# Attention heads of a hybrid transformer layer: 64-column value product and key projection in column pairs, row sums on GpSimd

## What is computed

```python
def mla_q(cq, q_norm_g, w_uq, cos, sin):
    q = (rms_norm(cq, q_norm_g) @ w_uq).reshape(B, S, MLA_HEADS, QK_NOPE + QK_ROPE)
    ...
def mla_kv(ckv, k_rope, kv_norm_g, w_ukv, cos, sin):
    kv = (rms_norm(ckv, kv_norm_g) @ w_ukv).reshape(B, S, MLA_HEADS, QK_NOPE + V_HEAD)
    k_nope, v = kv[..., :QK_NOPE], kv[..., QK_NOPE:]
    ...
def attend(q_nope, q_rope, k_nope, k_rope, v):
    s = jnp.einsum('bqhd,bkhd->bhqk', q_nope, k_nope) + jnp.einsum('bqhr,bkr->bhqk', q_rope, k_rope)
    p = jax.nn.softmax(s.astype(jnp.float32) * MLA_SCALE, axis=-1).astype(v.dtype)
    return jnp.einsum('bhqk,bkhd->bqhd', p, v)
```

## Time and profile before

| | us |
|---|---|
| median of 3 runs | 2931.52 (2930.42 to 2933.87) |
| profiled execution, its own time | 2926.87 |
| its span in the profile | 2925.0 |
| TensorE matmuls busy | 2750.9 (94%) |
| VectorE busy | 2183.4 (75%) |
| ScalarE busy | 1541.6 (53%) |
| GpSimd busy | 306.9 (10%) |

### The profile page before, as it was taken

One profiled execution on the slowest core, in us unless ns is written; L12 is line 12 of the kernel. 1 busy time (PEld: TensorE's weight loads), 2 busy tenths in 40 slices (PEclk: granted clock), 3 DMA queues, 4 the chain that ended last, 5 costly groups with the idle time before them and its releaser, 6 DMA issues. The chain is left out here.

```text
span 2925.0 us, 39328 instructions
## 1 busy us (share of the span) xinstructions
PE 2750.9 (94%) x13482; PEld 2111.5 (72%) x13482; DVE 2183.4 (75%) x2247; ACT 1541.6 (53%) x1486; POOL 306.9 (10%) x250
## 2 busy tenths in 40 slices
PE   5999998999998975999999999999999999999993
PEld 2765586678786544888888888888888888888882
DVE  1114357566662447999999999999999999999995
ACT  1212212333332113777777777777777777777774
POOL 0010000000001200111111111111111111111110
PEclk8999989999999987999999999999999999999996
DMA  6520002000002224666196699966966966669993
GB/s 252 195 101 1 1 0 74 6 5 6 3 1 80 88 90 174 201 201 201 29 337 205 207 378 378 378 205 216 363 201 215 359 201 202 233 205 377 376 335 136
DMA packets 223497, 527.53 MB, mean 180 GB/s; under 512 B 25938, under 2 KB 26195, under 8 KB 222323
## 3 DMA queue, kind: packets, MB, share of 16 engines
q1 hardware_dynamic: 206544, 475.31, 44.4%
q0 software_dynamic: 13968, 50.86, 7.4%
q10 hardware_dynamic: 2930, 0.62, 0.1%
HBM read 487.92 MB, written 38.81 MB: 180 GB/s over the span
## 5 line engine op out<-in xcount | busy, mean ns | idle before, releaser
L1883 DVE TENSOR_TENSOR wl<-w,wh 128x2048 fp32r<-128x2048 f32 x580 | 1301.4, 2284 | 26.9 <-ACT wh L1831 21.1
L1831 ACT ACTIVATE wh<-w 128x2048 fp32r<-128x2048 f32 x580 | 1111.7, 1917 | 291.1 <-PE PS L1744 291.1
L1744 PE MATMUL PS<-wh,xTh 128*128 128x512 f32 x1536 | 497.6, 405 | 4.0 <-DVE wl L1883 4.0
L1744 PE MATMUL PS<-wl,xTh 128*128 128x512 f32 x1536 | 474.9, 390 | 0.0
L1744 PE MATMUL PS<-wh,xTl 128*128 128x512 f32 x1536 | 474.3, 390 | 0.0
L1744 PEld LDWEIGHTS PS<-wh,xTh 128*128 128x128 f32 x1536 | 285.9, 189 | 68.2 <-DVE wl L1883 4.9
L1744 PEld LDWEIGHTS PS<-wl,xTh 128*128 128x128 f32 x1536 | 288.6, 188 | 61.8
L1744 PEld LDWEIGHTS PS<-wh,xTl 128*128 128x128 f32 x1536 | 288.6, 188 | 61.6
L1744 PE MATMUL PS<-wh,hTh 128*128 128x512 f32 x768 | 261.5, 421 | 0.0
L1723 POOL DMA_INDIRECT acc_dram<-hid,idxs x48 | 136.9, 2852 | 1089.9 <-DVE hid L1932 1089.9
L1744 PE MATMUL PS<-wh,hTl 128*128 128x512 f32 x768 | 241.0, 395 | 0.0
(11 more groups left out here) (329 smaller groups left out, 2993.1 us busy)
## 6 DMA issues: line engine op xcount, KB each, us to landing
w<-in_w_gu_dram SPq DMA_DIRECT2D x512, 512.0 KB, 9.1
w<-in_w_down_dram SPq DMA_DIRECT2D x128, 1024.0 KB, 10.5
later_wmod<-in_w_mod_dram SPq DMA_DIRECT2D x8, 2048.0 KB, 8.1
wmod<-in_w_mod_dram SPq DMA_DIRECT2D x8, 1024.0 KB, 13.7
w_mixer<-in_w_in_dram SPq DMA_DIRECT2D x8, 512.0 KB, 19.6
x<-in_x_dram SPq DMA_DIRECT2D x8, 512.0 KB, 3.4
w_out<-in_w_out_dram SPq DMA_DIRECT2D x1, 4096.0 KB
ox<-in_x_dram SPq DMA_DIRECT2D x8, 512.0 KB, 4.1
```

The source lines that it names most:

```text
L1744: mm = pe.matmul(PS[:, bank + g, :], op[:, k, :], ws[slot][:, kk, g, :], start=False, stop=(last and op is xs[1]))
L1831: act.activation(wh[c % SLOTS][:, :], w[c][:, :], ACT.Copy).then_inc(s_hi, 1)
L1883: dve.tensor_tensor(wl[c % SLOTS][:, :], w[c % NW][:, :], wh[c % SLOTS][:, :].bitcast(F32), ALU.subtract).then_inc(s_lo, 1)
```

## The change

The value product is turned round: the head's value tile (64 columns, now without the ones) is stationary and 512 columns of `probT` move; an even key tile writes output partitions 0 to 63, the odd one beside it 64 to 127. So each half ends with two partial sums, transposed. VectorE copies them to SBUF (`values_out`), and TensorE's `output_rows` adds and transposes them by a product with two stacked identities, and makes the row sums by a product of `acc` with a column of ones. `acc` is the sum of the ten `probT` tiles, made by nine additions on GpSimd for each half. `project_k` computes keys 0 to 639 in one column group and 640 to 1279 in the other, so `k_hi` and `k_lo` have two pieces. Exps wait until the old tile in their slot has been added. `max_rows(h,1)`, `max_hi(h,1)` and `max_lo(h,1)` move to later places, and the slots of the scores are new.

```diff
+            @block.gpsimd
+            def _(pool):
+                def add(h, half, op):
+                    done = 18 * h + (9 * half + op)
+                    pool.wait_ge(s_ex, h * NST + (NT * half + op + 2))
+                    if op:
+                        pool.wait_ge(s_acc, done)
+                        pool.tensor_tensor(acc[half][:, :], acc[half][:, :], probT[:, op + 1, :], ALU.add).then_inc(s_acc, 1)
+                    else:
+                        pool.tensor_tensor(acc[half][:, :], probT[:, 0, :], probT[:, 1, :], ALU.add).then_inc(s_acc, 1)
+                def body(h, j, more):
+                    for half in range(2):
+                        if not (isinstance(h, int) and h == 0):
+                            pool.wait_ge(s_ot, 2 * h + (half - 1))
+                        for op in range(9):
+                            add(h, half, op)
...
                 def k_hi(h, j):
                     act.wait_ge(s_kp, h + 1)
-                    act.activation(kTh[j][0:NOPE, :], flat[0:NOPE, 0:KEYS], ACT.Copy).then_inc(s_kh, 1)
+                    act.activation(kTh[j][0:NOPE, 0:KH], flat[0:NOPE, 0:KH], ACT.Copy)
+                    act.activation(kTh[j][0:NOPE, KH:], flat[NOPE:P, 0:KH], ACT.Copy).then_inc(s_kh, 1)
...
                         act.wait_ge(s_st, h * NST + (n + 1))
+                        if n >= NT or not (isinstance(h, int) and h == 0):
+                            act.wait_ge(s_acc, 18 * h + (9 * (n // NT) + max(n % NT, 1) - 9))
...
                 def body(h, j, more):
                     exps(h, 0, 8)
+                    max_hi(h, j, 1)
                     if more:
                         q_hi(h + 1, 1 - j)
                         k_hi(h + 1, 1 - j)
...
                     exps(h, NT + 7, NST)
-                    if more:
-                        max_hi(h + 1, 1 - j, 1)
...
+                def values_out(h, half):
+                    dve.wait_ge(s_pv, 2 * h + (half + 1))
+                    dve.tensor_copy(oT[:, :], PS[:, O0, :]).then_inc(s_ov, 1)
                 def output(h, half):
-                    dve.wait_ge(s_pv, 2 * h + (half + 1))
+                    dve.wait_ge(s_ot, 2 * h + (half + 1))
...
                 def body(h, j, more):
-                    max_lo(h, j, 1)
                     if not (isinstance(h, int) and h == 0):
+                        values_out(h - 1, 1)
                         output(h - 1, 1)
                     if more:
                         q_rope(h + 1)
...
                     mixer_square(h)
+                    max_lo(h, j, 1)
                     if more:
                         k_lo(h + 1, 1 - j)
-                        maxima(h + 1, 0, 3)
+                        maxima(h + 1, 0, 1)
+                    values_out(h, 0)
+                    if more:
+                        maxima(h + 1, 1, 3)
                     output(h, 0)
...
-                    for c, (lo, w) in enumerate(CH):
+                    for c, (lo, w) in enumerate(((0, 512), (512, KH - 512))):
                         for k in range(KVL // P):
-                            mm = pe.matmul(PS[0:NOPE, S0 + c, 0:w], wkh[j][:, k, :], m.ckvT[:, k, lo:lo + w],
-                                           start=(k == 0), stop=(k == KVL // P - 1))
+                            for e in range(2):
+                                mm = pe.matmul(PS[NOPE * e:NOPE * e + NOPE, S0 + c, 0:w], wkh[j][:, k, :], m.ckvT[:, k, KH * e + lo:KH * e + lo + w],
+                                               start=(k == 0), stop=(k == KVL // P - 1))
...
-                    pe.wait_ge(s_ex, h * NST + (NT * half + t + 1))
+                    pe.wait_ge(s_ex, h * NST + (NT * half + 2 * i + 2))
+                    for e in range(2):
+                        mm = pe.matmul(PS[VH * e:VH * e + VH, O0, :], v[j][:, 2 * i + e, :], probT[:, 2 * i + e, :],
+                                       start=(i == 0), stop=(i == NT // 2 - 1))
+                    if i == NT // 2 - 1:
+                        mm.then_inc(s_pv, 1)
+                def output_rows(h, half):
+                    pe.wait_ge(s_ov, 2 * h + (half + 1))
+                    pe.wait_ge(s_acc, 18 * h + (9 * half + 9))
                     for q in range(NQ // 2):
-                        mm = pe.matmul(outs[:, q, :], probT[:, t, q * P:(q + 1) * P], v[j][:, t, :],
-                                       start=(t == 0 and q == 0), stop=(t == NT - 1 and q == NQ // 2 - 1), skip_group_check=True)
+                        pe.matmul(outs[:, q, 0:VH], oT[:, q * P:(q + 1) * P], pair_i[:, :], start=True, stop=True)
+                    for q in range(NQ // 2):
+                        mm = pe.matmul(outs[:, q, VH:VH + 1], acc[half][:, q * P:(q + 1) * P], ones[:, :], start=True, stop=True)
+                    mm.then_inc(s_ot, 1)
...
                     if more:
                         project_q(h + 1, 1 - j)
+                    max_rows(h, 1)
+                    if not (isinstance(h, int) and h == 0):
+                        output_rows(h - 1, 1)
                     for n in range(8):
                         key_scores(h, j, n)
...
-                    todo = [(0, t) for t in range(NT)] + [(None, n) for n in range(NT, NST)] + [(1, t) for t in range(NT)]
-                    slot = {3: 0, 7: 1, 10: 2, 13: 3, 16: 4, 18: 5, 21: 6, 25: 7}
+                    todo = [(0, i) for i in range(NT // 2)] + [(None, n) for n in range(NT, NST)] + [(1, i) for i in range(NT // 2)]
+                    slot = {2: 0, 4: 1, 7: 2, 9: 3, 12: 4, 14: 5, 16: 6, 18: 7}
                     for n, (half, which) in enumerate(todo):
                         if more and n in slot:
                             scores(h + 1, 1 - j, slot[n])
-                        if more and n == 17:
+                        if n == 8:
+                            output_rows(h, 0)
+                        if more and n == 12:
                             max_rows(h + 1, 0)
...
-                    if more:
-                        max_rows(h + 1, 1)
```

More of the change, by code:

```diff
@@ L898, in phase_attention @@
             ("wkh0", [P, KVL // P, NOPE], F32), ("wkh1", [P, KVL // P, NOPE], F32),
-            ("negmax", [P, NQ], F32), ("rinv", [P, 2, NQ // 2], F32), ("cst", [P, SEQ], F32), ("qraw", [DQ, SEQ], F32), ("rtmp", [P, HALF], F32),
+            ("negmax", [P, NQ], F32), ("rinv", [P, 2, NQ // 2], F32), ("acc0", [P, HALF], F32),
+            ("pairI", [P, VH], F32), ("ones", [P, 1], F32), ("cst", [P, SEQ], F32), ("qraw", [DQ, SEQ], F32), ("rtmp", [P, HALF], F32),
             ("msv", [P, 4, MH], F32), ("msln", [P, MH], F32)])
-        m.attn, qTh0, qTh1, qTl0, qTl1, kTl1, wq0, wq1, wk0, wk1, negmax, rinv, cst, qraw, rtmp, msv, msln = items
+        m.attn, qTh0, qTh1, qTl0, qTl1, kTl1, wq0, wq1, wk0, wk1, negmax, rinv, acc0, pair_i, ones, cst, qraw, rtmp, msv, msln = items
         assert end <= m.R1
@@ L904, in phase_attention @@
             ("kTh0", [DQ + 1, KEYS], F32R), ("kTh1", [DQ + 1, KEYS], F32R), ("kTl0", [DQ + 1, KEYS], F32R)])
-        (probT, vall), at_end = m.run(end, [("probT", [P, NT, HALF], F32), ("vall", [P, NT, HEADS, VH + 1], F32)])
+        (probT, vall, acc1), at_end = m.run(end, [("probT", [P, NT, HALF], F32), ("vall", [P, NT, HEADS, VH], F32), ("acc1", [P, HALF], F32)])
+        oT = m.at("oT", [P, HALF], F32, m.tabs_at)
+        acc = (acc0, acc1)
+        KH = KEYS // 2
         assert at_end <= 229344
@@ L909, in phase_attention @@
         assert end + 4 * KVL // P * HEADS * VH <= m.R1 + 32768
-        (v0, v1), _ = m.run(m.after_w_out, [("v0", [P, NT, VH + 1], F32), ("v1", [P, NT, VH + 1], F32)])
+        (v0, v1), _ = m.run(m.after_w_out, [("v0", [P, NT, VH], F32), ("v1", [P, NT, VH], F32)])
         qTh, qTl, kTh, kTl, v, wqh, wkh = (qTh0, qTh1), (qTl0, qTl1), (kTh0, kTh1), (kTl0, kTl1), (v0, v1), (wq0, wq1), (wk0, wk1)
@@ L944, in _ @@
                 sp.wait_ge(s_wo, 16)
+            @block.gpsimd
[14 more added lines that the diff above has]
+                            add(h, half, op)
+                heads(pool, body)
             @block.scalar
@@ L994, in _ @@
                 max_hi(0, 0, 0)
-                max_hi(0, 0, 1)
                 def body(h, j, more):
                     exps(h, 0, 8)
+                    max_hi(h, j, 1)
                     if more:
@@ L1098, in _ @@
                 dve.wait_ge(s_krl, 2)
-                dve.memset(vall[:, :, :, VH:VH + 1], 1.0).then_inc(s_kr, 1)
+                dve.sem_inc(s_kr, 1)
+                for e in range(2):
+                    dve.tensor_copy(pair_i[64 * e:64 * e + VH, :], m.ident[64 * e:64 * e + VH, 64 * e:64 * e + VH])
+                dve.memset(ones[:, :], 1.0).then_inc(s_cs, 1)
                 dve.wait_ge(s_tab, 32)
@@ L1133, in _ @@
                 heads(dve, body)
+                values_out(HEADS - 1, 1)
                 output(HEADS - 1, 1)
@@ L2016, in build_program @@
         ("cs_tab", [P, NT, ROPE], F32), ("sn_tab", [P, NT, ROPE], F32)])
+    m.tabs_at = end - 2 * 4 * NT * ROPE
```

14 lines of the change are left out of this document (8 added, 6 removed).

## The result

The changed kernel took 2967.41 us (median of 4 runs, 2961.37 to 2977.76) against 2930.97 us (2926.19 to 2933.87) for the kernel before on the same chip: ratio 1.0130, 95% interval 1.0097 to 1.0162. It is slower by 36 us. The forecast was 2947, in a range of 2912 to 2970. Its profiled execution took 2969.58 us with a span of 2967.5.

A forecast was written before the change was run, and what follows sets the result against it. TensorE bounds the attention heads; the change moves the bound to VectorE's chain: 47.1 + 3.2 + 0.4 + 1.2 = 51.9 us a middle head. Six heads +18.8, head 0 +2, last -4.3, start -1.4: 2947 us, range 2912 to 2970.

The forecast's parts named there:

- The value product and the keys: TensorE per head: value product 8.6 us instead of 18.5, key projection 2.2 instead of 4.4; sum -8.4 with output rows.
- the forecast's likeliest case: Middle heads: bound moves to VectorE's chain, period 47.1, with contention and clock 51.9 us; total 2947; chance 0.47.
- the links: VectorE's chain of row maxima, each waiting for its scores: 2.44 us a link where nothing else stands between.
- The contention: VectorE operations waiting behind GpSimd's additions: 3.2 us a head on the way to the keys, 0.4 for q_lo and gate.
- The clock: Scores and two value pairs behind TensorE's 5 to 6 us gap may run at half speed: 1.2 us a head, 0 to 2.
- The last head: No scores chain, TensorE or GpSimd bound: 30.9 us plus 1 for GpSimd against 36.2 before, -4.3.
- Start and head 0: Stage start -1.4 us, from key projection and small operations; head 0, without output rows before it, 51.1 against about 49, +2.
- a small contention: Rival 1, middle heads: few VectorE operations wait and TensorE keeps its clock; period 47.3 to 48.2, 2914 to 2920; chance 0.27.
- one addition's time with the clock up: Rival 2, VectorE loses one addition in the whole train, clock stays: period 49.3, about 2931, no change; chance 0.15.
- TensorE as the bound: Rival 3, TensorE stays the bound because the assumed VectorE order is wrong: -8.4 x 8, 2865; chance 0.03.
- pairs that don't run side by side: Rival 4, value product needs 17 us, period above 56: 2980 or more; chance 0.03.
- the contention at its full price: Rival 5, the gate's small operations wait too and GpSimd is late at the last heads: 2968 to 2985; chance 0.05.

The follow-up runs named there:

- the filler: The changed kernel with 18 useless matmuls put into TensorE's 4.3 us wait for the second low part of the keys: 2950.62 us, 1.0063 of the kernel before.
- the reciprocal late: The changed kernel with the mixer's 3.34 us reciprocal moved behind the first maximum on VectorE: 2964.92 us, ratio 1.0069.
- the additions after the rotation: The changed kernel with mixer first and output late, GpSimd's first additions also waiting for the next head's rotated queries: 2911.79 us, ratio 0.9926.

## Why the prediction was right

**The value product and the keys, right.** Two pairs of tiles in 1.94 us (forecast 0.86 for each), key projection 2.38 (2.2), maxima rows and both kinds of output rows as the weight loads said. TensorE did stop being the bound, and the gain of 8.4 us a head was lost on VectorE's chain, as the forecast's likeliest case had it. That the period would fall only to 47.1 without contention and clock can be tested in two ways. With most additions left out, the four heads at the full clock took 48.3 us, of which 0.5 is the addition that was kept: 47.8. And with the parts that the runs isolate taken off the changed kernel's head (53.8 - 2.5 for the clock - 2.8 and 0.6 for GpSimd) it is 47.9. So the links are some 0.8 us a head longer than I had summed. Nearly all of it lies behind the keys; the way to the keys came out at 22.7 (25.5 - 2.8) against 22.75, with one slip in it: 8.1 and 0.75 make 8.85, not 9.05.

**The contention, right in size and mechanism.** Forecast 3.2 us on the way to the keys. Measured in the head shown, against the earlier trace rows: rotation 0.51 + 0.21, copy 0.77, gate's addition 1.08, small one 0.25, together 2.8. The keys were ready at 25.5 instead of the forecast 26. My picture of the train was half right: one copy and `L1102` paid, the second copy (0.17) and the square (0.67) not. The step that I had left open, whether a copy and an operation with one tensor and a constant are held, is settled: 0.19 became 0.96 and 0.42 became 1.50. The Trainium skill (SBUF — State Buffer, Who interferes with whom) says that a copy or an operation of this form, in a mode that uses two ports, contends with GpSimd for the pair of ports that the two engines share; the measurements agree, though not all seven operations of my upper end waited. In the last head, where GpSimd starts only at 918.51, `L1101` and `L1102` ahead of it took 0.68 and 0.42 again, as forecast. The addition itself was mis-sized: 1.28 us and 1.42 from one to the next, not 1.1, in proportion from 768 columns. In the middle heads that cost TensorE nothing, for it still lies within the cover of 2 us; in the last head it did.

**The clock, right in mechanism and wrong in size.** This is the term that failed in the middle heads. I took 1.2 us, between 0 and 2; the filler shows 2.5. It named the right work: two scores and two value pairs took 1.41, 3.68 and 1.38 us instead of the filler's 0.82, 1.94 and 0.85, together 2.9 us more. But I priced it as if VectorE's links hid half of that. The prediction's own walk had maximum 1 behind the copy of the values, and the copy behind the fifth pair, so nearly the whole lengthening lies on the chain. Six heads at 1.3 us more are 8 of the 11 us by which the middle heads were off. The remaining 3 us are the links (0.8 a head), less the 0.2 by which both terms for GpSimd together came out below 3.6.

**The last head, wrong.** Forecast -4.3, measured +2.1. Two terms failed here, the clock, which I had left at full speed, and the 1 us for GpSimd. (The items of the sum also add up to 29.9, not 30.9.) The clock first. In this head, in order of time:

```profile
913.15 1.81 PE L1258 MATMUL PS<-ones,acc 128*128 128x1 f32 x8
...
917.53 0.63 PE L1236 MATMUL PS<-qTh,kTh 97*128 97x512 f32 x1
...
933.27 0.78 PE L1236 MATMUL PS<-qTh,kTh 97*128 97x512 f32 x1
```

```profile
915.00:916.00 1.00, 1.00 (x3) 0.81 (x4) 0.96 (x3) 0.00 (x0) 0.00 (x0) 0.50 0.00 0
938.00:939.00 1.00, 1.00 (x4) 0.71 (x4) 0.00 (x0) 0.32 (x2) 0.86 (x2) 0.50 0.00 0
```

The key scores take 0.63 us each instead of 0.39, at a granted clock of 0.50, twice for some 7 us. Both times the fall comes in output rows that stand behind a wait. Ten and fourteen half-speed key score passes at 0.2 us more each, and the slow output rows, make 3 us for each stretch. But that is not the miss, for without these stretches the head is not 6 us shorter. With the filler, with the reciprocal late and with the additions after the rotation, TensorE and GpSimd have the same instructions in the last head as in the changed kernel, and the clock stayed at 1.00 for its first 31 us. It took 35.9 us in all three. The output rows in the middle and at the end of the head, with the filler:

```profile
912.23 1.08 PE L1256 MATMUL PS<-pairI,oT 128*128 128x64 f32 x8 [1.44 <-POOL acc L959]
...
926.26 1.94 PE L1256 MATMUL PS<-pairI,oT 128*128 128x64 f32 x8 [2.78 <-POOL acc L959]
```

TensorE waits 4.2 us for GpSimd's sums, and the last output rows, behind the longer wait, run at half the clock. Nine additions take 12.7 us, where I had counted 10.4. With most additions left out and the clock at 1.00 to the end, the head took 30.7 us, close to the sum without GpSimd. So the additions cost 5.2 us here (30.7 to 35.9, of which 1.6 are the last output rows at half the clock), where I had put 1, and the stretches of the changed kernel's trace 2.0 more (35.9 to 37.9): its slower TensorE waits only 0.61 us for the sums, so the two costs hide each other in part. The clock's part varies from run to run: one kernel took 34.3 us in one trace and 37.9 in the other.

**Start and head 0, right** (-2.6 and +2.5 against -1.4 and +2), head 0 by luck in part: the kernel before took 49.1 us for it in one trace and 47.5 in the other. **Behind the stage** I forecast nothing and the trace has +10.5, of which the section above shows only where it lies.

So the sign and the mechanism of the middle heads held, and the size did not. In the traces the forecast was 27 us short (42.5 against 15): 11 in the middle heads, 8 of them the clock, 6 in the last head, 4 of them the additions, 10 behind the stage. The medians lie 36.4 apart, so 6 us of that were the one execution's. The measured median lies 2.6 us inside the upper end of the range, and that end was not drawn for what lies behind the stage or for the last head: that it held is luck in part. Of the rivals, a small contention (2914 to 2920) fell with the first trace, and so did one addition's time with the clock up (2931), TensorE as the bound, and pairs that don't run side by side. Of the rival with the contention at its full price one part came true: GpSimd was late in the last head.

## What to carry to other kernels

When a change takes work off the engine that bounds, write out the in-order chain of the next engine link by link first, and look for long operations on it that nobody is waiting for. Here a reciprocal of 3.3 us and a wait for output rows stood ahead of the rotation, and moving them turned 1.3% slower into 0.8% faster. A gap that opens on TensorE can cost twice, once for itself and once for the slow clock behind it. In this kernel the clock fell behind every gap of over 4 us and behind some of 1.8 to 2.3, so price the work behind such a gap at half speed when the chain runs through it. Work given to GpSimd is free only while VectorE has no copy, no operation on a tensor and a constant, and none with two SBUF inputs beside it, or while another engine is later anyway. And its own train has to end in time where nothing else is left to cover it: in the last head it was GpSimd that TensorE waited for.

## What the runs showed of the hardware

- An fp32 operation on GpSimd that adds two tiles of 128x512 took 1.28 us, and 1.42 from one to the next in a train. Beside it a VectorE copy of 48 columns took 0.96 instead of 0.19 us, an addition of a constant over 512 columns 1.50 instead of 0.42. An operation in the train directly behind one that had waited kept its length (0.17 and 0.67).
- Two 64-column groups of fp32 matmuls with 512 columns run side by side: 8 half passes in 1.94 us at the full clock, 3.68 at half.
- TensorE's granted clock fell to 0.50 behind a gap of 4.2 to 4.3 us in the middle of a busy head in all seven heads of the changed kernel, for 6.8 us in five and 3.4 in two. Behind gaps of 2.0 to 2.3 us it fell in two of six heads, behind gaps of 1.7 to 1.8 in two of five, for 3.4 us each, and stayed at 1.00 in the others. It stayed at 1.00 when useless matmuls filled the gap, and it fell in output rows of 64 and 1 column behind waits of 0.6 to 1.7 us.
- The 48 scatters of one program took 2.85 us each in some runs, and up to nine of them 7.25 us (some 9.4) in others.
